# A Conformer kernel's opening: projection operands without the inverse root, root applied to the results, loads reordered, own taps in two banks

## Chip, cores, metric

The kernel runs on one core of one Trainium2 chip. Times are device microseconds (us) of one execution; the number that counts is the median of several runs. The profile is one further execution, recorded by the hardware profiler; its span goes from the first to the last instruction.

Engines: TensorE (PE, its weight loads PEld), VectorE (DVE), ScalarE (ACT), GpSimd (POOL) and SyncE (SP, which issues the transfers here).

## The reference, cut

Two blocks run one after the other on x of 512 tokens by 1024 features. All that the change touches is the first mixer of the first block, a Conformer convolution behind an RMS norm:

```python
u = rms_norm(h, conv_norm_g)                        # x * rsqrt(mean(x*x) + eps) * g
a = u @ w_pw1 + b_pw1                               # 1024 -> 2048
u = a[..., :D] * sigmoid(a[..., D:])                # gate
u = causal_depthwise_conv(u, dw_w, width 31) + dw_b
u = silu(layer_norm(u, ln_g, ln_b))
h = h + u @ w_pw2 + b_pw2
...                                                 # FFN, gate by projection, attention, second block
```

The root, rsqrt(mean(x*x) + eps), is one number for each token.

## The kernel before

Data lies transposed: features on the 128 partitions, tokens along the 512 columns, so x is 8 chunks of 128 x 512 (`h`). A float32 product is made of three matmuls in a faster format: each operand is cut into a rounded high part and the remainder as low part, and the product is high x high + low x high + high x low (lines 733, 734, 735). ACT rounds weights and operands, POOL subtracts for the low part of weights, DVE for the low part of operands.

Weights stream through a ring of four slots (`weight_raw`), 1 MB each. Slot j of `pw1` holds, for output chunk j, 128 columns for the value and 128 for the gate: two tiles of 8 x 3 matmuls each, in PSUM banks (`conv_tile`). Bank t is written again only when `tile_used` says so.

The opening, before: SP loads the 8 chunks of x, with the constants among them, then the params, then the first slots. ACT squares each chunk (line 3057), DVE adds the squares (2179), PE sums them over the partitions with a matmul against ones (904), ACT makes the inverse root with Ln and Exp (2709, 2712). Then `rms_apply`: for each chunk DVE multiplies h, gain and root into PSUM (1600), ACT rounds that to `u_hi` (2648), DVE subtracts for `u_lo` (1585, one operand in PSUM). PE starts on a chunk as its `u_lo` is there. While it waits, PE runs filler matmuls on constants (`keep_at_work`, line 1331) and small products for an attention bias table and a scalar lambda, whose results DVE copies out (2189 to 2195).

The convolution, 31 taps a channel, is split over engines for each chunk c: PE does 12 taps (16 in the last chunk) with diagonal weights (1352), on shifted copies that SP makes by DMA from the gated chunk (610); POOL builds the diagonals (2540). DVE does 12 own taps (10 in the last) in a chain in PSUM bank 6 (2236, 2238). ACT scales by a tap and POOL adds for the other 7 (5), the side taps (3105, 3110, 2536). For each chunk:

- ACT's sigmoid of the gate tile (2841), then DVE's gate (2222), which frees the two banks and lets SP, ACT and DVE start on the chunk;
- ACT's rounding of the slot after next (2640) and POOL's low half of it (2499);
- inside the next chunk's own taps, behind the fourth, DVE's sum of the three shares (`conv_finish`, 2247, 2249), which ACT squares for the layer norm (3090) and DVE adds up (2207, 2209).

Each engine works through its instructions in the order of the program; semaphores order them among each other. `link` makes DVE wait for the instruction just issued before it goes on; `link(..., 1)` lets one stay open.

Of the kernel before, what the change touches and what calls it, by code (L numbers as in the profile page):

```python
# [22 lines left out]
P = 128  # L23
# [27 lines left out]
BANKS = 4  # L51
HALF = P // 2
# [9 lines left out]
    ("conv_norm_g", 8), ("conv_b_pw1", 16), ("conv_dw_w", 8 * (CONV - OWN_FROM)), ("conv_tap_rows", SHIFTS * sum(TAP_GROUPS)), ("conv_dw_b", 8),  # L62
    ("conv_ln_g", 8), ("conv_ln_b", 8), ("conv_b_pw2", 8), ("attn_norm_g", 8),
    ("q_norm_g", 1), ("k_norm_g", 1), ("sub_norm_g", 1), ("lambda", 4),
# [5 lines left out]
for _name, _w in PARAM_WIDTHS:  # L70
    PARAM_AT[_name] = _n
    _n += _w
N_PARAMS = _n

CONST_WIDTHS = [("ident", P), ("flip", P), ("ones", P), ("ones64", P), ("key_fold", P), ("chunkmask", P),
                ("ahead", P), ("first_counts", 64), ("fold", 32), ("spread", QUARTER), ("eps", 2), ("zero", 1)]
# [4 lines left out]
N_CONSTS = _n  # L81
LATE_WIDTH = HEADS * P + 2 * S
# [151 lines left out]
def build(nc, a, out):  # L234
    stages, landed_due, tiles_after, split_no, slot_width, hi_free = plan_slots()
    n_slots = len(slot_width)
    with ExitStack() as ctx:
# [126 lines left out]
        diagonals = arena[:, DC * S:DC * S + group_base[DC] * P]  # L364
        side_base = [sum(SIDE_TAPS[:c]) for c in range(DC)]
# [5 lines left out]
        def conv_tile(t):  # L371

            return ps[:, t % BANKS]

# [47 lines left out]
        par_landed, con_landed = sem("par_landed"), sem("con_landed")  # L422
        p_landed = sem("p_landed")
# [114 lines left out]
        def _(sp):  # L538
            n = Tally()
            for c in range(DC):  # L540
                sp.dma_start(chunk(h, c), a["x_t"][c * P:(c + 1) * P]).then_inc(x_landed[c], 16)
                if c == 3:
                    sp.dma_start(con[:], a["consts"]).then_inc(con_landed, 16)
            sp.dma_start(par[:], a["params"]).then_inc(par_landed, 16)
# [47 lines left out]
            for j in range(RING):  # L592
                load("pw1", pair(a["conv_w_pw1"], a["conv_w_pw1"], 0, D), only=j)
                if j == 0:
                    sp.dma_start(v_sb[0:BUCKETS, 0:HEADS], a["rel_bias"]).then_inc(inputs_landed, 16)
                    sp.dma_start(v_sb[0:BUCKETS + 1, 8:648], a["bucket_of"]).then_inc(inputs_landed, 16)

            sp.wait_ge(bias_sb, 1)
            sp.dma_start(bias_rows, act[0:HEADS, 20 * S:20 * S + 640]).then_inc(bias_stored, 16)
# [12 lines left out]
            for c in range(DC):  # L612
                shift_copies(c)
                if c < DC - RING:
# [91 lines left out]
        def _(pe):  # L706
            n = Tally()
            pe.sem_inc(tile_used, BANKS)
            pe.wait_ge(con_landed, 16)
# [623 lines left out]
            keep_at_work(2, ps[:, 1])  # L1333
            rms_stat(adds=8)
            keep_at_work(3, ps[:, 1])
# [219 lines left out]
        def _(dve):  # L1555
# [671 lines left out]
            def conv_taps(c):  # L2227
# [13 lines left out]
                if c:  # L2241
                    square_sum(c - 1)
# [1166 lines left out]
```

## Time and profile before

| | |
|---|---|
| median of 3 runs | 2500.81 us (2500.45 to 2500.85) |
| the profiled execution's own time | 2501.13 us |
| its span | 2499.1 us |
| busy share PE / PEld | 98% / 79% |
| busy share DVE / ACT / POOL | 54% / 40% / 44% |
| HBM read | 269.72 MB, 109 GB/s over the span |

A row of the timeline gives the start, the time that it covers, engine, line, operation, tile written <- tiles read, how many instructions, and in brackets how long the engine sat idle before it and what released it. Busy times of PE overlap, since matmuls are pipelined.

### The profile page before, as it was taken

To read this page: it belongs to the slowest core of one execution; us is meant where nothing else is said; L and a number is where in the kernel's file an instruction comes from. 1 tells how busy PE (TensorE), PEld (TensorE's weight loads), DVE (VectorE), ACT (ScalarE), POOL (GpSimd) and SP (SyncE) were. 2 spreads that over 40 slices of the span, in tenths; PEclk is the share of its full clock that TensorE was granted. 3 is DMA by queue.
4 is the path that set the end of the run, shared out by engine and by line. 5 is a ranking of instruction groups with operands and counts; after the bars stand their busy time and mean duration, and the time that the engine had idled before them with its cause. 6 is when DMAs were issued, how large, how long until landed. Compare 5 with 4: busy or idle time off the path is not lost.

```text
span 2499.1 us, 31843 instructions
## 1 busy us (share of the span) xinstructions
PE 2457.9 (98%) x11794; PEld 1971.9 (79%) x11794; DVE 1355.7 (54%) x2128; ACT 987.5 (40%) x1386; POOL 1100.4 (44%) x555
## 2 busy tenths in 40 slices
PE   8999999999999999999999999999999999999998
PEld 5768888887777788888877878888888758888887
DVE  7856635635566465365338655551554465652553
ACT  5553222235565432223334254532344243532333
POOL 6944444444332344444443413544444313544443
PEclk9999999999999999999999999999999999999999
DMA  7635546533322364564352312324332222324322
GB/s 191 164 88 174 186 142 202 164 89 110 94 71 72 82 213 161 167 190 136 93 145 85 101 35 76 92 76 117 95 87 91 64 68 68 85 80 114 99 76 70
DMA packets 403321, 282.06 MB, mean 113 GB/s; under 512 B 10707, under 2 KB 382419, under 8 KB 403196
## 3 DMA queue, kind: packets, MB, share of 16 engines
q1 hardware_dynamic: 389372, 230.06, 32.7%
q10 hardware_dynamic: 13824, 50.34, 5.4%
q8 instruction: 77, 1.26, 0.2%
q14 instruction: 48, 0.39, 0.0%
HBM read 269.72 MB, written 2.12 MB: 109 GB/s over the span
## 4 chain that ended last, share of the span: by engine, by line
PE 91%; DVE 4%; ACT 3%; issue 1%; POOL 1%; DMA 1%; SPq 0%; DVEq 0%; ACTq 0%
PE ps L733 27%; PE ps L735 27%; PE ps L734 27%; PE ps L1511 1%; PE ps L1352 1%; PE ps L1120 1%; PE ps L1094 1%; PE ps L1233 1%; PE ps L1079 1%; PE ps L1082 1%; PE ps L1208 1%; DVE u_lo L1689 1%; PE ps L1453 0%; ACT weight_hi L2640 0%; PE ps L1222 0%
## 5 line engine op out<-in xcount | busy, mean ns | idle before, releaser
L2499 POOL TENSOR_TENSOR weight_lo<-weight_raw,weight_hi 128x1024 fp32r<-128x1024 f32 (+3 forms) x417 | 944.0, 2285 | 1315.3 <-ACT weight_hi L2640 1191.5
L735 PE MATMUL ps<-u_hi,weight_lo 128*128 128x512 f32 (+1 forms) x2456 | 929.7, 379 | 0.0
L733 PE MATMUL ps<-u_hi,weight_hi 128*128 128x512 f32 (+1 forms) x2248 | 879.6, 391 | 9.1 <-DVE u_lo L1585 2.2
L734 PE MATMUL ps<-u_lo,weight_hi 128*128 128x512 f32 (+1 forms) x2248 | 869.5, 387 | 0.0
L2640 ACT ACTIVATE weight_hi<-weight_raw 128x2048 fp32r<-128x2048 f32 (+2 forms) x213 | 363.1, 1705 | 571.4 <-PE ps L735 539.9
L735 PEld LDWEIGHTS ps<-u_hi,weight_lo 128*128 128x128 f32 x2456 | 462.1, 188 | 86.3
L733 PEld LDWEIGHTS ps<-u_hi,weight_hi 128*128 128x128 f32 x2248 | 422.4, 188 | 117.7 <-issue 15.8
L734 PEld LDWEIGHTS ps<-u_lo,weight_hi 128*128 128x128 f32 x2248 | 422.5, 188 | 86.2 <-issue 2.9
L735 PE MATMUL ps<-act_hi,weight_lo 128*128 128x512 f32 (+1 forms) x748 | 282.0, 377 | 0.0
L733 PE MATMUL ps<-act_hi,weight_hi 128*128 128x512 f32 (+1 forms) x704 | 269.8, 383 | 0.0
L734 PE MATMUL ps<-act_lo,weight_hi 128*128 128x512 f32 (+1 forms) x704 | 269.5, 383 | 0.0
L1585 DVE TENSOR_TENSOR act_lo<-tmp,act_hi 128x512 f32 (+1 forms) x88 | 160.4, 1823 | 98.4 <-ACT act_hi L2648 98.4
L1925 DVE SCALAR_TENSOR_TENSOR tmp<-ps,par,tmp 128x510 f32<-128x510 f32 (+1 forms) x176 | 119.7, 743 | 153.5 <-ACT tmp L2901 153.5
L735 PEld LDWEIGHTS ps<-act_hi,weight_lo 128*128 128x128 f32 x748 | 140.7, 188 | 25.6
L734 PEld LDWEIGHTS ps<-act_lo,weight_hi 128*128 128x128 f32 x704 | 132.4, 188 | 25.9
L733 PEld LDWEIGHTS ps<-act_hi,weight_hi 128*128 128x128 f32 x704 | 132.4, 188 | 25.8
L1854 DVE SCALAR_TENSOR_TENSOR ps<-arena,small,ps 128x512 f32<-128x512 f32 x168 | 118.7, 752 | 33.3 <-DMA arena<-in_ada_w 26.6
L2901 ACT ACTIVATE tmp<-ps,par 128x512 f32<-128x512 f32 x88 | 59.5, 681 | 166.3 <-PE ps L735 166.3
L2850 ACT ACTIVATE tmp<-tmp 128x512 f32<-128x512 f32 x60 | 37.9, 632 | 201.2 <-DVE tmp L1885 141.5
L1804 DVE TENSOR_TENSOR ps<-ps,tmp 128x512 f32<-128x512 f32 x32 | 22.4, 700 | 130.4 <-PE ps L735 130.4
L2648 ACT ACTIVATE act_hi<-tmp 128x512 f32 (+1 forms) x88 | 55.1, 626 | 82.8 <-DVE tmp L1932 62.1
L1932 DVE TENSOR_TENSOR tmp<-tmp 128x512 f32<-128x512 f32 x44 | 55.2, 1256 | 34.1 <-ACT tmp L2906 34.1
(335 smaller groups left out, 2683.7 us busy)
## 6 DMA issues: line engine op xcount, KB each, us to landing
weight_raw<-in_ffn_w_up SPq DMA_DIRECT2D x132, 512.0 KB, 5.2
arena<-in_ada_w ACTq DMA_DIRECT2D x96, 512.0 KB, 5.8
weight_raw<-in_ffn_w_down SPq DMA_DIRECT2D x64, 704.0 KB, 4.6
weight_raw<-in_ffn_w_gate SPq DMA_DIRECT2D x44, 512.0 KB, 4.0
weight_raw<-in_ev_w_in SPq DMA_DIRECT2D x10, 1024.0 KB, 5.6
weight_raw<-in_conv_w_pw SPq DMA_DIRECT2D x16, 512.0 KB, 6.6
weight_raw<-in_ple_w_gate SPq DMA_DIRECT2D x16, 512.0 KB, 3.8
weight_raw<-in_attn_w_qkv SPq DMA_DIRECT2D x16, 512.0 KB, 5.2
```

Of the source, the lines that this page charges most:

```text
L733: pe.matmul(bank, w[0], x[0], start=start, stop=False)
L734: pe.matmul(bank, w[0], x[1], start=False, stop=False)
L735: return pe.matmul(bank, w[1], x[0], start=False, stop=stop)
L1585: dve.tensor_tensor(lo, t, hi.bitcast(F32), ALU.subtract).then_inc(x_ready, 1)
L1854: ada_link(dve.scalar_tensor_tensor(acc, row, by, acc, ALU.mult, ALU.add), 1 - z)
L1925: link(dve.scalar_tensor_tensor(y[:, back:], bank[:, 0:S - back], tap, y[:, back:], ALU.mult, ALU.add), spare)
L1932: dve.tensor_tensor(sq[par_], act_tmp[par_], rinv[par_], ALU.mult).then_inc(t_ready, 1)
L2499: low_part = pool.tensor_tensor(w_lo[r][:, cols], raw[r][:, cols], w_hi(k0 + j)[:, cols].bitcast(F32), ALU.subtract)
L2640: sc.activation(w_hi(slot)[:, 0:width], raw[slot % RING][:, 0:width], ACT.Copy).then_inc(w_rounded, 1)
L2648: sc.activation(dst, src, ACT.Copy).then_inc(hi_done, 1)
L2850: sc.activation(t, t, func).then_inc(act_done, 1)
L2901: sc.activation(y, bank, ACT.Copy, scale=tap).then_inc(act_done, 1)
```

## The change

What it does:

- **Operands.** `u_hi` is h times gain, rounded by ACT straight from h; `u_lo` is h times gain less `u_hi`, by DVE. Neither needs the root. Squares and their sum go on beside them, the running sum in PSUM.
- **Root on results.** PE sums the squares after chunk 0's products; ACT makes the root into SBUF. DVE multiplies both tiles of each chunk by it (`conv_scale`): the gate tile goes to SBUF, where ACT takes the sigmoid, the value tile stays in its bank. The biases still come after that, in sigmoid and gate.
- **Weights and loads.** Halves of slot 0 and 1 land on semaphores of their own and are rounded and split as they come; chunk 0 and 1's first tiles run their matmuls with high weights before those with low weights. SP's order is: a first cut of the params, first half slot, two chunks of x, a first cut of the constants, chunk 2, second half slot, the other chunks, slot 1, then the rest of params and constants.
- **Own taps** alternate between PSUM banks 6 and 3, with one instruction left open, and are added at the end. So the projection's tiles use three banks instead of four.
- **Moved**: the bias products behind chunk 1's tiles on PE, their copies behind the own taps of chunk 0 on DVE; lambda's product first on PE; all filler matmuls ahead of the products go; POOL builds two tables of diagonals ahead of the loop instead of five, and one in each of six rounds instead of three.

The diff, cut to its core:

```diff
-            for c in range(DC):
+            def input_chunk(c):
                 sp.dma_start(chunk(h, c), a["x_t"][c * P:(c + 1) * P]).then_inc(x_landed[c], 16)
...
+            sp.dma_start(par[:, 0:PARAMS_FIRST], a["params"][:, 0:PARAMS_FIRST]).then_inc(par_first_landed, 16)
+            half_slot(0, 0)
+            input_chunk(0)
+            input_chunk(1)
+            sp.dma_start(con[:, 0:CONSTS_FIRST], a["consts"][:, 0:CONSTS_FIRST]).then_inc(ones_landed, 16)
+            input_chunk(2)
+            half_slot(0, 1)
+            for c in range(3, DC):
+                input_chunk(c)
+            half_slot(1, 0)
+            half_slot(1, 1)
+            sp.dma_start(par[:, PARAMS_FIRST:], a["params"][:, PARAMS_FIRST:]).then_inc(par_landed, 16)
+            sp.dma_start(con[:, CONSTS_FIRST:], a["consts"][:, CONSTS_FIRST:]).then_inc(con_landed, 16)
...
-            keep_at_work(2, ps[:, 1])
-            rms_stat(adds=8)
-            keep_at_work(3, ps[:, 1])
...
+                pe.wait_ge(first_rounded, 1)
                 for k in range(DC):
                     pe.wait_ge(x_ready, n.next(x_ready))
-                    if k == 0:
+                    high_passes(0, 0, k)
+                    if k == 3:
+                        pe.wait_ge(w_rounded, 1)
+                        for q in range(3):
+                            high_passes(0, 1, q)
                         pe.wait_ge(first_low, 1)
-                    first_product(0, k)
-                    if k == 3:
-                        slot_of("pw1", Step(0))
                         for q in range(3):
-                            first_product(1, q)
+                            low_pass(0, 0, q)
                     if k >= 3:
-                        first_product(1, k)
-                pe.wait_ge(lam_exp, 1)
-                pe.wait_ge(bias_sb, 1)
+                        high_passes(0, 1, k)
+                        low_pass(0, 0, k)
+                    if k == 6:
+                        pe.wait_ge(w_ready, 1)
+                        for q in range(6):
+                            low_pass(0, 1, q)
+                    if k >= 6:
+                        low_pass(0, 1, k)
+                rms_stat(adds=8)
...
+            for c in range(DC):
+                dve.wait_ge(hi_done, i0 + c + 1)
+                dve.scalar_tensor_tensor(chunk(u_lo, c), chunk(h, c), pcol("conv_norm_g", c), chunk(u_hi, c).bitcast(F32),
+                                         ALU.mult, ALU.subtract).then_inc(x_ready, 1)
+                dve.wait_ge(squared, q0 + c + 1)
+                if c == 0:
+                    dve.tensor_copy(square_sum_bank, sq[0]).then_inc(summed, 1)
+                else:
+                    dve.wait_ge(summed, c)
+                    dve.tensor_tensor(sum2 if c == DC - 1 else square_sum_bank, square_sum_bank, sq[c % 2], ALU.add).then_inc(summed, 1)
...
+            def conv_scale(c):
+
+                dve.wait_ge(tile_done, t0 + 2 * c + 2)
+                dve.tensor_tensor(act_tmp[c % 2], conv_tile(2 * c + 1), rinv[0], ALU.mult).then_inc(conv_scaled, 1)
+                link(dve.tensor_tensor(conv_tile(2 * c), conv_tile(2 * c), rinv[0], ALU.mult))
...
-                own, y = ps[:, 6], chunk(conv_out, c)
-                for t in taps:
-                    x = cin[:, t:t + S]
-                    if t == taps[0]:
-                        link(dve.tensor_scalar(own, x, tap(t), None, ALU.mult))
+                own, y = (ps[:, 6], ps[:, 3]), chunk(conv_out, c)
+                for k, t in enumerate(taps):
+                    x, acc = cin[:, t:t + S], own[k % 2]
+                    last = t == taps[-1]
+                    if k < 2:
+                        link(dve.tensor_scalar(acc, x, tap(t), None, ALU.mult), 1)
                     else:
-                        link(dve.scalar_tensor_tensor(y if t == taps[-1] else own, x, tap(t), own, ALU.mult, ALU.add))
-                    if t == taps[3] and c:
+                        link(dve.scalar_tensor_tensor(y if last else acc, x, tap(t), acc, ALU.mult, ALU.add), 0 if last else 1)
+                    if k == 3 and c:
                         conv_finish(c - 1)
                 if c:
                     square_sum(c - 1)
+                if c < DC - 1:
+                    conv_scale(c + 1)
+                link(dve.tensor_tensor(y, own[len(taps) % 2], y, ALU.add))
...
+            split_half(0, 0)
+            sc.wait_ge(par_first_landed, 16)
             for c in range(DC):
                 sc.wait_ge(x_landed[c], 16)
+                sc.activation(chunk(u_hi, c), chunk(h, c), ACT.Copy, scale=pcol("conv_norm_g", c)).then_inc(hi_done, 1)
                 if c >= 2:
                     sc.wait_ge(summed, c - 1)
                 sc.activation(sq[c % 2], chunk(h, c), ACT.Square).then_inc(squared, 1)
+                if c == 2:
+                    split_half(0, 1)
...
+            split_half(1, 0)
             link.begin(0)
             sc.wait_ge(stat_done, n.next(stat_done))
...
+            inverse_root(ps[:, 4], 1.0 / D, eps_rms, rinv[0])
+            split_half(1, 1)
```

Where the order of instructions changes, at three places. In the names, `weight_raw_49` and `_51` are slots 0 and 1, `weight_hi_57` and `_58` the two buffers of rounded weights, `weight_lo_50` and on the low parts; `tmp`, `act`, `arena` are working tiles, `small` and `par` columns of scalars.

ACT in the opening before, from the root to the first rounding of a whole slot:

```order
L2709 ACTIVATE tmp<-ps,con 128x512
L2712 ACTIVATE ps<-tmp 128x512
L3066 ACTIVATE weight_hi_57<-weight_raw_49 128x1024
L2648 ACTIVATE u_hi<-ps 128x512
L3066 ACTIVATE weight_hi_57<-weight_raw_49 128x1024
...
L2648 ACTIVATE u_hi<-ps 128x512 x3
L3082 ACTIVATE small<-ps 128x2
L2841 ACT_TABLE_LOAD
L2841 ACTIVATE tmp<-ps,par 128x512
L2640 ACTIVATE weight_hi_57<-weight_raw_53 128x2048
```

ACT there in the changed kernel, from the last chunk of x on (what it waits for in brackets):

```order
L3114 ACTIVATE u_hi<-h,par 128x512 [waits x_landed7]
L3117 ACTIVATE tmp<-h 128x512 [waits summed]
L3122 ACTIVATE small<-ps 128x2 [waits lam_mm]
L3108 ACTIVATE weight_hi_58<-weight_raw_51 128x1024 [waits half_landed1]
L2768 ACTIVATE tmp<-ps,con 128x512 [waits stat_done]
L2771 ACTIVATE tmp<-tmp 128x512 [waits a_chain]
L3108 ACTIVATE weight_hi_58<-weight_raw_51 128x1024 [waits weights_landed1]
L2889 ACT_TABLE_LOAD
L2889 ACTIVATE tmp<-tmp,par 128x512 [waits conv_scaled]
L2699 ACTIVATE weight_hi_57<-weight_raw_53 128x2048 [waits weights_landed2,tile_done,par_landed]
```

The root (2768, 2771) has moved behind the operands of all chunks; a half of slot 1 and the table load now stand between it and the first sigmoid.

DVE, in chunk 1's round before, from the sums of chunk 0 to the gate of chunk 2:

```order
L2247 TENSOR_TENSOR ps<-ps,arena 128x512 [waits pe_taps_done,d_chain]
L2249 TENSOR_TENSOR arena<-ps,act 128x512 [waits side_added,d_chain]
L2238 SCALAR_TENSOR_TENSOR ps<-act,par,ps 128x512 [waits d_chain] x7
L2238 SCALAR_TENSOR_TENSOR arena<-act,par,ps 128x512 [waits d_chain]
L2207 COPY ps<-tmp 128x512 [waits squared,d_chain]
L2222 SCALAR_TENSOR_TENSOR act<-ps,par,tmp 128x512 [waits d_chain,act_done,tile_done]
```

And in the changed kernel:

```order
L2301 TENSOR_TENSOR ps<-ps,arena 128x512 [waits pe_taps_done,d_chain]
L2303 TENSOR_TENSOR arena<-ps,act 128x512 [waits side_added,d_chain]
L2289 SCALAR_TENSOR_TENSOR ps<-act,par,ps 128x512 [waits d_chain] x7
L2289 SCALAR_TENSOR_TENSOR arena<-act,par,ps 128x512 [waits d_chain]
L2252 COPY ps<-tmp 128x512 [waits squared,d_chain]
L2262 TENSOR_TENSOR tmp<-ps,tmp 128x512 [waits d_chain,tile_done]
L2263 TENSOR_TENSOR ps<-ps,tmp 128x512
L2296 TENSOR_TENSOR arena<-ps,arena 128x512 [waits d_chain]
L2272 SCALAR_TENSOR_TENSOR act<-ps,par,tmp 128x512 [waits act_done,d_chain]
```

Two scalings (2262, 2263) and the sum of the two banks (2296) are new ahead of the gate; the wait for PE's tiles has moved from the gate to the first scaling.

POOL ahead of the rounds and in the first, before:

```order
L2547 TENSOR_TENSOR weight_lo_50<-weight_raw_49,weight_hi_57 128x1024 x2
L2540 TENSOR_TENSOR arena<-con,par 128x384 x2
L2499 TENSOR_TENSOR weight_lo_52<-weight_raw_51,weight_hi_58 128x2048
L2540 TENSOR_TENSOR arena<-con,par 128x384 x3
L2499 TENSOR_TENSOR weight_lo_54<-weight_raw_53,weight_hi_57 128x2048
L2536 TENSOR_TENSOR act<-act 128x512 x6
L2499 TENSOR_TENSOR weight_lo_56<-weight_raw_55,weight_hi_58 128x2048
```

And in the changed kernel:

```order
L2608 TENSOR_TENSOR weight_lo_50<-weight_raw_49,weight_hi_57 128x1024 x2
L2608 TENSOR_TENSOR weight_lo_52<-weight_raw_51,weight_hi_58 128x1024 x2
L2600 TENSOR_TENSOR arena<-con,par 128x384 x2
L2559 TENSOR_TENSOR weight_lo_54<-weight_raw_53,weight_hi_57 128x2048
L2596 TENSOR_TENSOR act<-act 128x512 x6
L2600 TENSOR_TENSOR arena<-con,par 128x384
L2559 TENSOR_TENSOR weight_lo_56<-weight_raw_55,weight_hi_58 128x2048
```

Three of the tables (2540, now 2600) have moved from ahead of the first round into rounds.

## Rows read from the trace of the kernel before

**Rows 1.** The page's head.

```profile
span 2499.1 us, 31843 instructions
```

**Rows 2.** Timeline of the opening: start, us covered, engine, line, operation.

```profile
0.75 1.28 ACT L2652 ACT_TABLE_LOAD   x1 [0.75 <-PEq L3400]
...
3.46 1.27 ACT L3057 ACTIVATE tmp<-h 128x512 f32<-128x512 f32 x2 [1.43 <-DMA h<-in_x_t]
...
13.71 0.69 ACT L2709 ACTIVATE tmp<-ps,con 128x512 f32<-128x512 f32 x1 [2.12 <-PE ps L904]
...
15.49 1.06 ACT L3066 ACTIVATE weight_hi<-weight_raw 128x1024 fp32r<-128x1024 f32 x1 [0.46 <-DMA weight_raw<-in_conv_w_pw]
...
16.62 4.71 POOL L2547 TENSOR_TENSOR weight_lo<-weight_raw,weight_hi 128x1024 fp32r<-128x1024 f32 x2 [16.17 <-ACT weight_hi L3066]
...
19.12 0.47 PE L733 MATMUL ps<-u_hi,weight_hi 128*128 128x512 f32 x1 [0.21 <-POOL weight_lo L2547]
...
27.23 0.67 DVE L2189 COPY act<-ps 8x512 f32<-8x512 f32 x1
...
29.13 0.15 DVE L2195 TENSOR_SCALAR small<-par 128x1 f32<-128x1 f32 x1
```

**Rows 3.** Timeline of DVE in the convolution's rounds.

```profile
32.49 0.75 DVE L2222 SCALAR_TENSOR_TENSOR act<-ps,par,tmp 128x512 f32<-128x512 f32 x1 [2.73 <-ACT tmp L2841]
...
44.89 0.75 DVE L2222 SCALAR_TENSOR_TENSOR act<-ps,par,tmp 128x512 f32<-128x512 f32 x1 [1.95 <-ACT tmp L2841]
45.90 0.76 DVE L2236 TENSOR_SCALAR ps<-act,par 128x512 f32<-128x512 f32 x1 [0.26 <-DVE act L2222]
...
50.83 5.50 DVE L2238 SCALAR_TENSOR_TENSOR ps<-act,par,ps 128x512 f32<-128x512 f32 x7 [0.34 <-DVE arena L2249]
...
59.06 0.75 DVE L2236 TENSOR_SCALAR ps<-act,par 128x512 f32<-128x512 f32 x1 [0.24 <-DVE act L2222]
...
126.33 0.75 DVE L2222 SCALAR_TENSOR_TENSOR act<-ps,par,tmp 128x512 f32<-128x512 f32 x1 [0.92 <-ACT tmp L2841]
```

**Rows 4.** Timeline of POOL in the same rounds.

```profile
34.23 4.62 POOL L2499 TENSOR_TENSOR weight_lo<-weight_raw,weight_hi 128x2048 fp32r<-128x2048 f32 x1 [3.76 <-ACT weight_hi L2640]
38.82 8.49 POOL L2536 TENSOR_TENSOR act<-act 128x512 f32<-128x512 f32 x6
...
60.31 0.84 POOL L2540 TENSOR_TENSOR arena<-con,par 128x384 f32<-128x384 f32 x1
```

**Rows 5.** Timelines of ACT, PE and DVE at the end of the convolution.

```profile
125.54 0.69 ACT L2841 ACTIVATE tmp<-ps,par 128x512 f32<-128x512 f32 x1 [1.00 <-PE ps L735]
...
135.50 3.64 PE L1352 MATMUL ps<-act,arena 128*32 128x512 f32 x32 [1.07 <-DMA act<-act]
...
139.21 0.70 DVE L2247 TENSOR_TENSOR ps<-ps,arena 128x512 f32<-128x512 f32 x1 [1.53 <-PE ps L1352]
```

**Rows 6.** Timeline of DVE elsewhere: neighbours that don't wait for each other.

```profile
195.60 0.70 DVE L1580 TENSOR_TENSOR ps<-ps,tmp 128x512 f32<-128x512 f32 x1
196.21 0.75 DVE L1816 SCALAR_TENSOR_TENSOR u_lo<-h,par,u_hi 128x512 fp32r<-128x512 f32 x1
...
247.88 1.41 DVE L1854 SCALAR_TENSOR_TENSOR ps<-arena,small,ps 128x512 f32<-128x512 f32 x2 [0.15 <-DVE ps L1852]
```

**Rows 7.** Timelines of POOL and DVE where line 1816 meets a split.

```profile
185.80 5.23 POOL L2499 TENSOR_TENSOR weight_lo<-weight_raw,weight_hi 128x1024 fp32r<-128x1024 f32 x2 [6.26 <-ACT weight_hi L2640]
...
186.89 1.88 DVE L1816 SCALAR_TENSOR_TENSOR u_lo<-h,par,u_hi 128x512 fp32r<-128x512 f32 x1
...
188.70 2.89 DVE L1816 SCALAR_TENSOR_TENSOR u_lo<-h,par,u_hi 128x512 fp32r<-128x512 f32 x1
```

**Rows 8.** Fillers on PE, ns min/median/max; one product in the chain that ended last.

```profile
L1331 PE MATMUL ps<-con x12: 592/593/1219, 8.1 to 18.3; 128*128 128x512 f32 x12
...
30.95 0.23 PE ps L733
```

**Rows 9.** Stretches: busy us of the engines, clock, DMA share, GB/s.

```profile
16.00:22.00 6.00, 5.41 (x18) 2.41 (x17) 5.77 (x10) 4.80 (x8) 5.38 (x3) 1.00 1.19 290
```

More of the change, by code:

```diff
@@ new lines, in conv_slots @@
+                        low_pass(0, 0, k)
[6 more added lines that the diff above has]
+                rms_stat(adds=8)
+                pe.wait_ge(first_rounded, 2)
+                for k in range(DC):
+                    high_passes(1, 0, k)
+                pe.wait_ge(first_low, 2)
+                for k in range(DC):
+                    low_pass(1, 0, k)
@@ L2712, in inverse_root @@
                 sc.activation(to if root is None else root, to, ACT.Exp, scale=-0.5).then_inc(done, 1)
-            def rms():
-                link.begin(0)
-                sc.wait_ge(stat_done, n.next(stat_done))
-                inverse_root(ps[:, 4], 1.0 / D, eps_rms, rinv[0])
-                n.take(x_ready, DC)
-                for c in range(DC):
-                    sc.wait_ge(t_ready, n.next(t_ready))
-                    high(chunk(u_hi, c), sq[c % 2])
             def ln(eps, src, func, gain, shift):
@@ L3057, in _ @@
                 sc.activation(sq[c % 2], chunk(h, c), ACT.Square).then_inc(squared, 1)
+                if c == 2:
+                    split_half(0, 1)
+            n.take(x_ready, DC)
+            sc.wait_ge(lam_mm, 1)
+            sc.activation(lam[:, 2:4], ps[:, 3, 0:2], ACT.Exp).then_inc(lam_exp, 1)
+            split_half(1, 0)
             link.begin(0)
             sc.wait_ge(stat_done, n.next(stat_done))
-            sc.wait_ge(con_landed, 16)
-            inverse_root(ps[:, 4], 1.0 / D, eps_rms, sum1, root=ps[:, 5])
-            def split_half(slot, z, done=None):
-                cols = slice(z * SLOT // 2, (z + 1) * SLOT // 2)
-                sc.wait_ge(landed[slot], landed_due[slot])
-                half = sc.activation(w_hi(slot)[:, cols], raw[slot][:, cols], ACT.Copy)
-                if done is not None:
-                    half.then_inc(done, 1)
-            split_half(0, 0, first_rounded)
-            n.take(x_ready, DC)
-            for c in range(DC):
-                sc.wait_ge(t_ready, n.next(t_ready))
-                high(chunk(u_hi, c), ps[:, 6 + c % 2])
-                if c == 0:
-                    split_half(0, 1, w_rounded)
-                if c == 2:
-                    split_half(1, 0)
-                if c == 4:
-                    split_half(1, 1, w_rounded)
-            sc.wait_ge(bias_mm, 1)
-            sc.activation(lam[:, 2:4], ps[:, 3, 0:2], ACT.Exp).then_inc(lam_exp, 1)
+            inverse_root(ps[:, 4], 1.0 / D, eps_rms, rinv[0])
+            split_half(1, 1)
             s0 = n.take(summed, DC - 1)
```

171 lines of the change are left out of this document (94 added, 77 removed).

## The prediction, on record before the result

> **What bounds the kernel now.** I read the page first: one core, a span of 2499.1 us [rows 1], TensorE (PE) busy for 98% of it. The diff ends with the Conformer convolution, about the first 140 us; nothing behind it changes but its place in time. So I read that stretch engine by engine, and the reader should see two things.
>
> First, the opening. The first product starts at 19.12 us [rows 2], behind squares, the inverse root on ScalarE (ACT) and a scaled copy per chunk. That is the idle time the change goes for.
>
> Second, what follows. From the gate of chunk 0 at 32.49 to that of chunk 7 at 126.33 [rows 3] the stage is a relay over four engines, each nearly full. PE needs 48 products of 0.23 us [rows 8] and 24 taps a chunk (32 of them took 3.64 [rows 5], so 2.7), 13.8. POOL needs a split (4.6), six side sums (8.45) and in some chunks a table of diagonals (0.8): 13.05 to 13.85 [rows 4]. VectorE (DVE) needs 13.16 where it waited for nothing (45.90 to 59.06) [rows 3]. The mean round was (126.33 - 44.89)/6 = 13.57. An opening that is 10 us shorter is therefore worth 10 us only if DVE and POOL start 10 us earlier too and need no more per chunk.
>
> After the gate of chunk 7 come the shifted copies, PE's last taps at 135.50 (1.07 us of waiting for DMA) and the last sum at 139.21 [rows 5]: 12.9 us behind the gate. The change leaves that tail alone, so **I forecast the gate of chunk 7** and carry its shift to the end. Its sigmoid waited 1.00 us for PE [rows 5]: PE is the bound there today.
>
> **The opening, step by step.** The first half slot of weights now goes ahead of x. Chunk 0 of x, first in the queue today, was being read at 3.46 [rows 2]. The half slot is 512 KB where that chunk is 256, and weights moved at 290 GB/s [rows 9]: 0.9 us more, and some 0.7 for the small transfer ahead of it and its shorter rows. That makes 5.1 us, an estimate; the bounds are 4.1 (no transfer in the way) and 8 (it lands no sooner than a later transfer does under load). ACT rounds it in 1.06 [rows 2]: 6.2. POOL then takes 2.36 for the low half (4.71 for two) [rows 2]: until 8.55.
>
> Here is the first catch. Before, DVE's low part of the operand read PSUM and one SBUF tile. Now it reads h and u_hi, both in SBUF, in the form of line 1816. Where that form met POOL's split (POOL from 185.80), it took 1.88 and 2.89 us and ended after each POOL instruction [rows 7]; alone it takes 0.75 [rows 6]. I take it as blocked: u_lo(0) ends at 9.3, and the first product starts there, 9.8 us earlier than today. (Bounds: never blocked, start 8.0.) DVE then spends 0.67 + 0.61 a chunk [rows 6]: u_lo(2) ends at 11.7. POOL's second half runs 11.7 to 14.05, and u_lo(3) is blocked again, to 14.85. u_lo(7) ends near 20.
>
> The second catch: until u_lo(3), PE has only 6 of chunk 0's 48 products to do; 42 remain, 42 x 0.23 = 9.7 us, to 24.5. The filler matmuls that ran ahead of the products are gone. Today the first of those lasted 1219 ns and the rest 592 [rows 8]: PE's first work after idling ran at half rate, 1.2 instead of 2.4 GHz, though the clock column does not show it. I charge 8 of the 42 at twice 0.23 (nearest row: about four such fillers), +1.6, hence 26.1; bounds 0 and 20 of them (+4).
>
> Only then comes the sum over partitions, since PE does chunk 0's products first: two matmuls of the fillers' kind (592 ns each, overlapping [rows 8]), 1.0 to 27.1; Ln and Exp at 0.69 [rows 2], 28.5. ACT then has the second half of slot 1 to round (1.0, to 29.5) and the table load of the sigmoid, 1.28 [rows 2], which today falls into an idle stretch: 30.7. DVE's scaling of both tiles (1.3) hides under those. Sigmoid 0.69, gate of chunk 0 at **31.4, against 32.49**. Of 9.8 us, 1.1 are left.
>
> **The rounds.** DVE's own taps alternate between two banks. In one bank each waits for the one before: 5.50 us for seven, 0.79 apart [rows 3]. Two of the same form on two banks took 1.41 together [rows 6], so 0.67 apart; that pair is the nearest row and I take it (bounds 0.61 and 0.79). Eleven gaps a chunk shrink by 0.12: -1.3. Added a chunk: two scalings, 0.61 + 0.73 (the second is waited for), and the sum of the two banks, 0.73: +2.07. DVE's round becomes 13.16 - 1.3 + 2.07 = 13.9.
>
> Chunk 0: gate 31.4, taps begin 1.0 later as today, 11 x 0.67 + 0.79 = 8.2 to 40.6, scalings 1.3, sum 0.73, and the bias copies, which ran 27.23 to 29.28 in idle time [rows 2] and now stand ahead of the gate, 2.05: gate of chunk 1 at 44.75, against 44.89 [rows 3]. Six rounds of 13.9: gate of chunk 7 at 128.15, against 126.33. **The sum is +1.8 us**, or +0.2 with the clock up at once.
>
> Cover for the rest: PE is no longer in the way. Chunk 1's tiles end near 38, its taps of chunk 0 at 42.6 once the copies land, and with 13.8 a chunk it has chunk 7's tiles at about 123, three before DVE asks. The move to three banks costs nothing while PE leads thus. POOL begins slot 2 at 33.6 (ACT's split behind the sigmoid), 34.23 today after 3.76 of waiting [rows 4]; but three diagonal tables that were built in that gap now stand inside the loop, +2.4. Its rounds are 13.85: chunk 6's sums start at 33.6 + 4.6 + 6 x 13.85 = 121.3 and end at 129.8. ACT's last product for them is released three adds of 1.42 earlier, 125.6, with sigmoid 7 behind it to 126.9: 1.2 us of slack before the gate. So POOL is a second bound, nearly as late as DVE: a faster DVE alone gains at most those 1.2 us. Reordered params and constants land by 20 (5.2 MB ahead at 290 GB/s from about 2 us on [rows 9]) and are needed at 30; moved bias products cost PE 1 us under its lead.
>
> The profiled execution took 2501.13 with 2.0 us outside its span; the runs' median is 2500.81. 2501.13 + 1.8 gives 2502.9, less 0.3 for the median, **2502.6 us**.
>
> **A rule against the change.** The two banks rest on 1.41 for a pair [rows 6]. The Trainium skill, page VectorE: DVE Perf Modes, section The DRAIN you can't avoid, says that the next op starts only when the pipe is empty, and that leaving out semaphores doesn't shorten that. By it the second bank would gain nothing. The pair here speaks against it; if it held, the time would be that of the third rival.
>
> **The rivals.**
> - *The forecast*: DVE's round and the late root eat the gain; 2502.6, its own range 2500 to 2506. Chance 0.63.
> - *Faster opening*: u_lo isn't held by POOL, PE is at full clock, the half slot lands 1 us sooner. u_lo(3) ends at 11.3, PE's products near 21, gate of chunk 0 at 26.3. POOL's chain, from about 28.4, then binds: gate of chunk 7 at 28.4 + 4.6 + 83.1 + 4.3 + 1.3 = 121.7 at best, -4.6. For it: POOL's own 185.80 row is only one meeting. Against it: both instructions there were late. 2496 to 2500; chance 0.15. Beyond -5 it would need POOL's rounds shorter as well, by moving 2.4 us of tables into slack that isn't there.
> - *Two banks don't overlap*: the taps stay 0.79 apart, DVE's round is 15.2, and 1.3 us more in chunk 0: 44.75 + 1.3 + 6 x 15.2 = 137.3, +11, so 2512. Slower is decided from a gap of about 0.72 on (5 us = 0.05 x 11 x 7 plus the 1.8). Against it: the pair; for it: an additional tile to finish, and the waits between. Chance 0.12.
> - *Late first weights*: the half slot shares its engines with x and lands 2 to 3 us later, and PE stays at half rate through most of chunk 0. All behind shifts: 2505 to 2508. Chance 0.10.
>
> **Numbers.** From no change a measurement of this kernel can tell about 0.2%, 5 us: below 2495.8 or above 2505.8. Faster 0.07 (the end of the second case and what I don't see), same 0.78, slower 0.15 (the third case and part of the last). The range of eight in ten leaves out the third rival and the far end of the second: 2498 to 2508.
>
> **What would show it.** In the profile after: first product near 9 us, u_lo of 2 us or more beside POOL's halves, the statistic near 26, gate of chunk 0 near 31, chunk 1's near 45, rounds of 13.9 on DVE with hardly a wait for PE, PE with some idle before the shifted copies, POOL full. The forecast is wrong if DVE's low parts run through POOL's splits, if own taps stand 0.6 or 0.79 apart, or if the first half slot lands far from 5 us.

## The result, and the profile after

The changed kernel takes 2504.51 us (median of 20 runs, 2502.60 to 2506.65), the kernel before 2500.65 (20 runs, 2500.17 to 2502.21): a ratio of 1.0015, 95% interval 1.0008 to 1.0022. It is 3.9 us slower and inside the range. The profiled run is the fastest of the 20: 2502.60, with a span of 2500.6 [rows 1]. A profile shows one run, so where the other 2 us of the median went can't be read from it.

The opening of the changed kernel, engine by engine (start, us covered, engine, line, operation, and in brackets the idle time before it and what ended it):

```profile
5.25 1.06 ACT L3108 ACTIVATE weight_hi<-weight_raw 128x1024 fp32r<-128x1024 f32 x1 [3.22 <-DMA weight_raw<-in_conv_w_pw]
...
6.38 2.36 POOL L2608 TENSOR_TENSOR weight_lo<-weight_raw,weight_hi 128x1024 fp32r<-128x1024 f32 x1 [5.94 <-ACT weight_hi L3108]
11.59 2.45 POOL L2608 TENSOR_TENSOR weight_lo<-weight_raw,weight_hi 128x1024 fp32r<-128x1024 f32 x1 [2.85 <-ACT weight_hi L3108]
...
7.04 2.25 DVE L2221 SCALAR_TENSOR_TENSOR u_lo<-h,par,u_hi 128x512 fp32r<-128x512 f32 x1 [3.54 <-ACT u_hi L3114]
12.33 2.25 DVE L2221 SCALAR_TENSOR_TENSOR u_lo<-h,par,u_hi 128x512 fp32r<-128x512 f32 x1
...
9.44 0.76 PE L1394 MATMUL ps<-u_hi,weight_hi 128*128 128x512 f32 x1 [1.87 <-DVE u_lo L2221]
14.64 0.79 PE L1394 MATMUL ps<-u_hi,weight_hi 128*128 128x512 f32 x1 [1.55 <-DVE u_lo L2221]
16.51 0.63 PE L1394 MATMUL ps<-u_hi,weight_hi 128*128 128x512 f32 x1
16.93 0.63 PE L1395 MATMUL ps<-u_lo,weight_hi 128*128 128x512 f32 x1
19.75 0.39 PE L1395 MATMUL ps<-u_lo,weight_hi 128*128 128x512 f32 x1
19.98 0.40 PE L1399 MATMUL ps<-u_hi,weight_lo 128*128 128x512 f32 x1
26.60 1.02 PE L930 MATMUL ps<-tmp,con 128*128 128x512 f32 x2
```

The first product starts at 9.44 instead of 19.12 [rows 2]. Both long u_lo end 0.55 us after the GpSimd split that runs beside them; the other six take 0.73 or 0.74. From 14.64 to 19.5 the products stand 0.43 apart, then 0.23. So the sum over partitions is taken at 26.60, and gate 0 comes only 0.4 us sooner than before [rows 3], as the timeline of VectorE shows:

```profile
32.09 0.75 DVE L2272 SCALAR_TENSOR_TENSOR act<-ps,par,tmp 128x512 f32<-128x512 f32 x1 [1.76 <-ACT tmp L2889]
...
43.32 0.68 DVE L2236 COPY act<-ps 8x512 f32<-8x512 f32 x1
44.03 0.28 DVE L2237 COPY act<-ps 8x128 f32<-8x128 f32 x1
44.35 1.25 DVE L2239 TENSOR_TENSOR small<-small 128x1 f32<-128x1 f32 x1
...
46.32 0.75 DVE L2272 SCALAR_TENSOR_TENSOR act<-ps,par,tmp 128x512 f32<-128x512 f32 x1 [0.35 <-DVE small L2241]
...
51.70 4.71 DVE L2289 SCALAR_TENSOR_TENSOR ps<-act,par,ps 128x512 f32<-128x512 f32 x7 [0.34 <-DVE arena L2303]
...
59.99 0.75 DVE L2272 SCALAR_TENSOR_TENSOR act<-ps,par,tmp 128x512 f32<-128x512 f32 x1
...
128.38 0.75 DVE L2272 SCALAR_TENSOR_TENSOR act<-ps,par,tmp 128x512 f32<-128x512 f32 x1
...
141.17 0.70 DVE L2301 TENSOR_TENSOR ps<-ps,arena 128x512 f32<-128x512 f32 x1 [1.70 <-PE ps L1378]
```

Seven own taps take 4.71 instead of 5.50 [rows 3]. Each round, gate to gate, is 13.68, six times. The last sum is 1.96 us later than in [rows 5]. In the table of waits over 44 to 127 us, VectorE waits for nobody but itself, and ScalarE's sigmoid waits for VectorE's scaling (us in total, times, longest):

```profile
DVE act L2272 <- DVE small L2241: 0.3, 1, 0.3
...
ACT tmp L2889 <- DVE tmp L2262: 4.5, 5, 1.4
```

### The profile page after: what moved, and what is told of

Same layout as the page of the kernel before. It is cut to its first block, busy times and chain, and to the rows that moved or that the text cites. A ratio compares the mean times of both kernels' runs of the same rounds, so it can differ in the third digit from the quotient of the medians.

```text
span 2500.6 us, 31829 instructions
## 1 busy us (share of the span) xinstructions
PE 2454.9 (98%) x11782; PEld 1971.0 (79%) x11782; DVE 1358.3 (54%) x2144; ACT 988.4 (40%) x1386; POOL 1101.2 (44%) x556
## 4 chain that ended last, share of the span: by engine, by line
PE 87%; DVE 7%; ACT 3%; issue 2%; POOL 1%; DMA 0%; SPq 0%; DVEq 0%; ACTq 0%
PE ps L759 26%; PE ps L760 26%; PE ps L761 26%; DVE ps L2289 1%; PE ps L1563 1%; PE ps L1146 1%; PE ps L1120 1%; PE ps L1259 1%; PE ps L1105 1%; PE ps L1108 1%; PE ps L1234 1%; DVE u_lo L1726 1%; PE ps L1505 0%; ACT weight_hi L2699 0%; DVE ps L2287 0%
## 5 line engine op out<-in xcount | busy, mean ns | idle before, releaser
L761 PE MATMUL ps<-u_hi,weight_lo 128*128 128x512 f32 (+1 forms) x2432 | 919.3, 378 | 0.0
L759 PE MATMUL ps<-u_hi,weight_hi 128*128 128x512 f32 (+1 forms) x2224 | 869.2, 391 | 8.5 <-POOL weight_lo L2559 2.0
L760 PE MATMUL ps<-u_lo,weight_hi 128*128 128x512 f32 (+1 forms) x2224 | 859.0, 386 | 0.0
L760 PEld LDWEIGHTS ps<-u_lo,weight_hi 128*128 128x128 f32 x2224 | 417.9, 188 | 85.2 <-issue 2.9
```

Source lines behind the costliest of these rows:

```text
L759: pe.matmul(bank, w[0], x[0], start=start, stop=False)
L760: pe.matmul(bank, w[0], x[1], start=False, stop=False)
L761: return pe.matmul(bank, w[1], x[0], start=False, stop=stop)
```

## The experiments

All but one are edits of the changed kernel, and all compute the reference in full; a filler is a matrix product whose result nobody reads. Medians are of 11 runs each (6 for the single bank). "Gate 7" and "last sum" are those of the profiled run, 128.38 and 141.17 in the changed kernel. The kernel before was run again beside each group of these runs and took 2500.64 to 2501.17, so a difference of half a microsecond between medians of different groups says nothing.

**The sum of squares ahead of the second tile's low products.**

```diff
+                    if k == DC - 1:
+                        rms_stat(adds=8)
+                        pe.wait_ge(w_ready, 1)
+                        for q in range(DC):
+                            low_pass(0, 1, q)
-                    if k == 6: ...
-                    if k >= 6: ...
-                rms_stat(adds=8)
```

> The sum of squares goes to TensorE as soon as it is made (20.2 us in the changed kernel's trace), ahead of the sixteen products that complete the second tile, instead of behind all of chunk 0's products (26.6 us). My theory (the convolution ends where VectorE's unbroken rounds of 13.68 us end, and these start at gate 0, which waits for the late root): root about 23, table load about 24 to 25, gate 0 at about 28.5 (was 32.09); gate 1 only 2 to 2.5 us earlier (it was 46.32), since TensorE's fourth tile, at 38.6, then holds the scaling; gate 7 at about 126 (was 128.38), median 2.0 to 2.5 us below the changed kernel's. Rival, TensorE's rounds (13.81 us) bind: gate 7 gains no more than 1 us. Rival, GpSimd's rounds (13.8 us) bind: its second-slot split moves forward with the root, so about 2 us too, but VectorE would then wait at its gates.

2502.91 (2501.88 to 2504.34), 1.6 below the changed kernel. The sum was taken at 24.73, not soon after 20.2, when its operand is made: TensorE, still behind its operands after the slow products, comes to it no sooner. Gate 0 stood at 30.23 (expected 28.5), gate 7 at 126.58, 1.8 sooner. The last sum stood at 140.85, only 0.3 sooner: something behind gate 7 took the rest.

**Bias copies on ScalarE, lambda operations in VectorE's last wait.**

```diff
-                if c == 0:
-                    bias_copies()
...
+            lambda_values()
             conv_finish(DC - 1)
...
+                    if i == 3 and c == 1:
+                        sc.wait_ge(bias_mm, 1)
+                        link(sc.activation(act[0:HEADS, 20 * S:21 * S], ps[0:HEADS, 7], ACT.Copy))
+                        sc.activation(act[0:HEADS, 21 * S:21 * S + P], ps[0:HEADS, 4, 0:P], ACT.Copy).then_inc(bias_sb, 1)
```

> The two copies of the bias products go from VectorE's path ahead of gate 1 to ScalarE, inside its side taps of chunk 1, and the three small operations on lambda to VectorE's wait for the last taps. My theory (VectorE's rounds bind from gate 0 on): gate 1 at 43.3 to 43.6 (was 46.32), gate 7 at 125.5 to 126.5 (was 128.38), median 2 to 3 us below the changed kernel's, or as much of that as TensorE's slack (about 1.7 us at the tiles of chunk 2) leaves. Rival, GpSimd binds: gate 1 earlier, but a wait of that size appears at gates 2 to 4, and gate 7 and the end stay within 0.5 us.

2504.02 (2503.34 to 2505.11). Gate 1 came at 44.55, yet gate 7 at 128.16: my theory missed, the rival holds (counted from gate 0, which was 0.36 later in this run, gate 7 gained 0.58). In the table of waits (44 to 127 us) ScalarE's wait for VectorE's scaling is gone: VectorE now waits for ScalarE, and ScalarE for nobody but GpSimd:

```profile
DVE ps L2252 <- ACT tmp L3132: 1.2, 4, 0.5
...
ACT act L3154 <- POOL act L2593: 36.9, 18, 5.6
```

**Fillers ahead of the first product.** Three of ones by ones, five on the half slot.

> TensorE is given matrix products without use from about 1.5 us on (three of ones by ones, then five on the first rounded half slot), up to the first product of the projection at 9.44 us; nothing else is changed. If the half rate of its first products (0.43 us apart until 19.3, 0.23 after) is what stands behind the late root: the products are 0.23 apart from the first on, the sum of squares is taken at 23 to 24 (was 26.6), gate 0 is at 29 to 30 (was 32.09), and the median is 1.5 to 2.5 us below, with a narrower spread of runs (the changed kernel's 20 runs lie 4 us apart, those before 2 us) if the spread comes from the moment at which the rate rises. Rival, the rate isn't set by what the engine did before, or the operands' arrival holds it: gate 0 within 0.5 us of 32.09 and the spread unchanged.

2502.58 (2500.95 to 2503.93), 1.9 below. No product stood 0.43 apart any more, but the fillers waited for the ones to land (7.39) and held the first product until 13.21, so the sum was taken at 24.97, gate 0 at 30.48 and gate 7 at 126.84. The runs still lay 3 us apart (4 in the changed kernel): the spread isn't made in the opening alone.

**One bank.** The own taps as in the kernel before, without the sum of two banks.

> VectorE's own taps go back into one bank, each waiting for the one before, without the sum of two banks at the end; the rest of the change stays. My theory (independent operations stand 0.66 apart, dependent ones 0.79, and VectorE's rounds bind): a round is 9 to 10 steps of 0.12 to 0.13 longer and one sum of 0.7 shorter, so 14.1 to 14.4 instead of 13.68, and gate 7 is 3 to 5 us later: median 3 to 5 us above the changed kernel's. Rival, two banks don't overlap: rounds 0.7 shorter, median up to 5 us lower. Rival, another engine binds: under 1 us of difference, with waits at the gates in the place of the difference.

2510.25 (2508.56 to 2510.87), 5.7 above. Seven taps took 5.50 again, and the round was 14.64: 0.96 longer, not the 0.4 to 0.7 that I expected: the taps cost 1.47 a round, and dropping the sum of the banks saved only 0.49 of its 0.73, since the gate then waits 0.25 for the scaling ahead of it. Two banks do overlap. The 5.7 us are not the rounds alone: this run's taps of chunk 7 took 6.50 us, for a reason that the next run shows.

**Two fillers ahead of the taps of chunk 7.** The run with the sum moved had shown where its gain went. TensorE's rows at the end of the convolution, first of the changed kernel, then of the one with the bias copies moved:

```profile
133.73 1.13 PE L936 MATMUL ps<-arena,con 128*128 128x512 f32 x2 [0.85 <-DVEq L2306]
137.38 3.64 PE L1378 MATMUL ps<-act,arena 128*32 128x512 f32 x32 [2.52 <-DMA act<-act]
```

```profile
133.49 1.13 PE L936 MATMUL ps<-arena,con 128*128 128x512 f32 x2 [0.35 <-DVEq L2304]
137.27 6.48 PE L1378 MATMUL ps<-act,arena 128*32 128x512 f32 x32 [2.65 <-DMA act<-act]
```

The same 32 taps took 3.64 and 6.48. The stretches of the second one give the reason (us, PE busy with its count, granted clock, DMA share, GB/s):

```profile
128.00:135.00 7.00, 6.27 (x14) 1.00 0.58 120
135.00:139.00 4.00, 1.73 (x11) 0.65 0.92 275
139.00:143.00 4.00, 4.00 (x24) 0.50 0.49 181
```

The clock fell to its lower level, 1.2 of 2.4 GHz, in TensorE's wait for the shifted copies, and the taps ran at it.

```diff
                 chunk_sums(0, DC - 1)
+                keep_at_work(2, ps[:, 1])
                 pe_taps(DC - 1)
```

> The changed kernel with two matrix products without use between TensorE's last chunk sum and its taps of chunk 7 (where it waited 2.52 us for the shifted copies, after 0.85 us ahead of that sum); nothing else is changed. Theory A: in most runs, though not in the changed kernel's profiled one (the fastest of its 20), TensorE's granted clock falls during this wait, as it shows in the profiles of four experiments (0.50 to 0.71 there, and the 32 taps take 5.2 to 6.5 us instead of 3.64). Then the clock stays at 1.00, the taps take 3.6 to 3.7 us, the last sum follows gate 7 by 12.8 us, and the median falls to 2502.3 to 2503.2 (from 2504.5), with the runs within about 2 us of each other. Theory B: the spread comes from elsewhere (the opening's clock, the landing of transfers): median within 0.5 us of 2504.5, runs 4 us apart.

2503.15 (2502.18 to 2504.74), 1.4 below the changed kernel, runs 2.6 us apart. The clock stayed at 1.00, the taps took 3.64, the last sum came 12.74 behind gate 7. Theory A.

**The same two fillers in the kernel before.**

> The kernel before with the same two products without use ahead of the taps of chunk 7. There TensorE waited 1.07 us in that place, and its taps ran at the full clock. Theory A: little or nothing to gain, 0 to 0.7 us, so the difference between this one and the changed kernel with the same products is that of VectorE's rounds alone, about 2 us. Theory B: no difference for either.

2501.59 (2500.98 to 2503.12) against 2500.82 (2499.61 to 2502.68): nothing to gain there; the 0.8 more lies inside the interval of the ratio (0.9994 to 1.0012). Its TensorE waits 1.07 us in that place [rows 5].

**Tables ahead.** GpSimd builds five ahead of the loop again.

> GpSimd builds five of the tap tables ahead of the loop, as the kernel before did, and the last three behind the sums of chunks 1 to 3; nothing else is changed. Theory (GpSimd's rounds of 13.8 us don't hold the end; VectorE's of 13.68 do, and TensorE's of 13.81 are next): its split of the second slot begins some 2.5 us later (was 34.00) and TensorE's tiles of chunk 2 or 3 may wait for it by up to 1 us, which VectorE's slack at the tiles covers; gate 7 within 0.3 us of 128.38, and the median within 0.7 us of 2504.5. Rival (GpSimd binds): the two tables moved out of the later rounds bring chunk 6's sums forward by 1 to 2 us and the end with them, or its later start sets the tiles back and the end by 1 to 2.5 us.

2505.03 (2503.34 to 2505.52), gate 7 at 128.61, both as my theory had it. The split of slot 2 began at 36.01, gate 1 waited 1.51 for its sigmoid, and VectorE's rounds went on from there.

**All of these together,** with fillers from 1.5 us on and the last half slot's rounding ahead of the root.

> The changed kernel with all that the runs so far favour: products without use on TensorE from 1.5 us to the first product, without the wait for the ones ahead of them (four of ones by ones, three on the first rounded half slot), the sum of squares behind the last chunk's first five products, the last half slot's rounding ahead of the root, the bias copies on ScalarE with the three small lambda operations in VectorE's last wait, and two products without use ahead of the taps of chunk 7. Theory (three engines have almost the same round: VectorE 13.68, GpSimd 13.8, TensorE 13.81; each of these edits alone meets the next engine, together they move all three): first products 0.23 apart from 9.5 on, sum of squares at about 21, gate 0 at 25.5 to 27, gate 1 at 38.5 to 40.5, gate 7 at 121 to 123.5 with TensorE's rounds as the bound, last sum 12.8 us behind it, at 134 to 136 (before 139.21, changed 141.17); median 2496 to 2498.5, below both kernels. Rival (the arrival of the weights holds the tiles of chunks 1 to 3 once the engines are earlier): gate 7 not before 125, median 2499.5 to 2501.

2504.27 (2501.41 to 2504.82): a miss, gate 0 at 31.96. Three of the 11 runs took 2501.4 to 2501.6, the others 2504.0 to 2504.8. The stretches of the opening of one of the latter (columns as above):

```profile
8.00:12.00 4.00, 2.77 (x10) 1.00 1.08 372
12.00:14.00 2.00, 0.73 (x2) 1.00 1.16 316
14.00:16.00 2.00, 0.82 (x2) 0.58 1.18 302
16.00:20.00 4.00, 4.00 (x10) 0.50 1.10 332
...
22.00:24.00 2.00, 2.00 (x10) 1.00 1.20 290
```

The fillers had brought the clock up, and it fell again while operands came one by one, the last wait 2.05 us for u_lo of chunk 3. At the other end the subtraction for lambda took 2.72 us in VectorE's last wait, and the last sum came 14.24 behind gate 7. What ran beside it was a GpSimd split, not a sum as a later expectation says; the two end within 0.02 us of each other:

```profile
138.64 2.72 DVE L2246 TENSOR_TENSOR small<-small 128x1 f32<-128x1 f32 x1
...
136.78 4.56 POOL L2566 TENSOR_TENSOR weight_lo<-weight_raw,weight_hi 128x2048 fp32r<-128x2048 f32 x1 [0.77 <-ACT weight_hi L2706]
```

**Fillers ahead of the taps of chunk 0 as well** (six of 0.23 us, and the two ahead of chunk 7's).

> The changed kernel with the two products without use ahead of the taps of chunk 7, as in the run with these alone (median 2503.15), and six of 0.23 us ahead of the taps of chunk 0, where TensorE waits 1.8 us and where the granted clock fell in three of the profiles (0.88 to 0.91 over 42 to 56 us). Theory: both places of the lost clock are covered; the 24 taps of chunk 0 take 2.78 us, gate 7 follows gate 0 by 96.3 us, and the median is 2502.3 to 2503.0. Rival: what is lost at the taps of chunk 0 is covered by TensorE's slack later: median as in the run with the last fillers alone, 2503.15 within 0.3.

2502.68 (2500.36 to 2503.86). The taps took 2.78 and 3.64, gate 7 came 96.34 behind gate 0. Against 2503.15 that is 0.5, which two medians with this spread don't settle.

**The filled opening alone,** with 3, 3 and 8 fillers behind the products of chunks 0 to 2.

> Only the opening is filled: products without use on TensorE from 1.5 us to the first product (without the wait for the ones), and 3, 3 and 8 of them behind the products of chunks 0, 1 and 2, where TensorE otherwise waits for the next operands (in the run with all edits the granted clock rose, fell to 0.50 at 14 us behind a wait of 2.05 us, and came back at 21). Theory: clock 1.00 from 9 us on, no product 0.43 apart, sum of squares at 21.5 to 23 (was 26.60), gate 0 at 27 to 28.5 (was 32.09); gate 1 at 41 to 43, gate 7 at 123.5 to 126, as TensorE's rounds (13.81) let it; median 2500 to 2502. Rival: the clock falls all the same, gate 0 within 1 us of 32.

2502.30 (2501.54 to 2504.15), 2.2 below. The clock held (1.00 in every stretch to 26 us) and no product was 0.43 apart, but gate 0 stood at 30.34 (expected 27 to 28.5), since the sum came at 24.83, not 21.5 to 23: u_lo of chunk 3 still ended at 15, and TensorE had 42 products to do from there. Gate 7 was at 126.29. The taps of chunk 7 took 5.91 at a clock of 0.50, behind 3.33 us of waiting: an earlier convolution loses more there.

**All, mended.** The edits of the run with all together, the filled opening just shown, and four fillers ahead of the taps of chunk 0. The subtraction is written as an operation on one tensor and stands in VectorE's wait for the root:

```diff
-                link(dve.tensor_tensor(lam[:, 4:5], lam[:, 3:4], lam[:, 2:3], ALU.subtract))
+                link(dve.tensor_scalar(lam[:, 4:5], lam[:, 3:4], lam[:, 2:3], None, ALU.subtract))
```

> The filled opening (with the fillers between the first chunks' products), the sum of squares behind the last chunk's first five products, the last half slot's rounding ahead of the root, the bias copies on ScalarE, the lambda operations in VectorE's wait for the root with the subtraction as an operation on one tensor (as one on two tensors it took 2.72 us in VectorE's last wait, next to a running GpSimd sum), four fillers ahead of the taps of chunk 0 and two ahead of those of chunk 7. Theory: sum of squares at 20.5 to 21.5, gate 0 at 25.5 to 27, gate 1 at 38 to 40, then TensorE's rounds of 13.81: gate 7 at 120.5 to 123, last sum at 133 to 136 (before 139.21), median 2495.5 to 2498.5, 2 to 5 us below the kernel before. Rival: the weights of the later slots or GpSimd hold the tiles, gate 7 not before 124.5, median 2499 to 2501.

2498.51 (2497.93 to 2500.05) against 2500.64: ratio 0.9990, 0.9981 to 0.9999. Gate 0 at 28.82, gate 7 at 124.38, last sum at 137.18: less than expected, with gate 7 close to the rival's 124.5 (GpSimd holds it, as the table below shows), but below both kernels. The subtraction took 0.21, beside a running split.

**And the second half's low part behind the last u_lo.**

```diff
                     pool.wait_ge(rounded, j + 1)
+                    if z and not j:
+                        pool.wait_ge(x_ready, DC)
```

> The version with all edits (median 2498.51) with one more: GpSimd takes the low part of the second half slot only once VectorE has written the last of u_lo, so that u_lo of chunk 3 runs beside no GpSimd operation; TensorE takes the eight low products of the second tile last, behind the sum of squares, and has 3 instead of 8 products without use behind chunk 2. Theory (the 2.25 to 2.31 us of u_lo of chunk 0 and of chunk 3, against 0.73 of the others, are a wait for the GpSimd operation that runs beside them): u_lo of chunk 3 takes 0.73 and ends at 13.2 (was 14.78), u_lo of chunk 7 at 18.3 (was 19.8), u_lo of chunk 0 stays at 2.25; the sum of squares is taken at 21 to 22 (was 24.27), gate 0 is at 25.5 to 27 (was 28.82), and TensorE ends chunk 0's products at about 24 (was 25.2), which carries 1 us to the end: median 2497 to 2498. Rival (a wait of its own, such as the landing of chunk 3, sets those 2.25 us): u_lo of chunk 3 stays at 2.2 us and the median goes up by the second half's delay, to 2499 or more.

**2496.50** (2496.29 to 2497.48) against 2500.79 (2500.39 to 2502.83): ratio 0.9982, 0.9973 to 0.9991. It is 8 us below the changed kernel and 4.3 below the one before, with the narrowest spread of all. VectorE's u_lo of chunks 0 and 3, and its waits over 44 to 127 us:

```profile
7.47 2.27 DVE L2232 SCALAR_TENSOR_TENSOR u_lo<-h,par,u_hi 128x512 fp32r<-128x512 f32 x1 [4.00 <-ACT u_hi L3124]
...
12.78 0.73 DVE L2232 SCALAR_TENSOR_TENSOR u_lo<-h,par,u_hi 128x512 fp32r<-128x512 f32 x1
```

```profile
DVE tmp L2270 <- PE ps L761: 2.3, 4, 1.4
```

With no split beside it, u_lo of chunk 3 takes 0.73; chunk 0's, which still has one, 2.27. The run also moves the second tile's eight low products behind the sum of squares, so the 2.0 us against the run before it belong to both. The sum was taken at 21.41, gate 0 was at 25.96, gate 7 at 122.58. VectorE now waits for TensorE's tiles.

## Why the prediction came out as it did

**Three chains set gate 7.** In every version that keeps the changed kernel's work in its rounds, gate 7 is the latest of three sums: VectorE's, gate 1 and six rounds of 13.68 (82.1); GpSimd's, its split of slot 2 and 93.8; TensorE's, its taps of chunk 0 (plus what the clock cost them beyond 2.78) and 85.2. The first constant is from the changed kernel, the second from the run with the bias copies moved, the third from the last run; the other rows test them. The starts for the changed kernel:

```profile
34.00 4.63 POOL L2559 TENSOR_TENSOR weight_lo<-weight_raw,weight_hi 128x2048 fp32r<-128x2048 f32 x1
...
41.77 2.78 PE L1378 MATMUL ps<-act,arena 128*32 128x512 f32 x24 [1.83 <-DMA act<-act]
```

| version | VectorE | GpSimd | TensorE | gate 7 seen |
|---|---|---|---|---|
| changed kernel | **128.4** | 127.8 | 127.0 | 128.38 |
| sum of squares early | **126.6** | 125.9 | 124.8 | 126.58 |
| bias copies moved | 126.6 | **128.2** | 127.2 | 128.16 |
| fillers ahead of first product | 126.5 | 126.2 | **126.8** | 126.84 |
| two fillers ahead of chunk 7 | 127.9 | 127.4 | **128.2** | 128.16 |
| both places filled | **127.8** | 127.2 | 126.2 | 127.83 |
| all together | 126.0 | **127.5** | 126.3 | 127.53 |
| filled opening alone | **126.3** | 126.0 | 124.6 | 126.29 |
| all, mended | 122.9 | **124.4** | 123.8 | 124.38 |
| and the late half | 120.1 | 121.5 | **122.6** | 122.58 |

The runs with one bank and with five tables ahead have other rounds and aren't in it. The first product came 9.7 us sooner, but the three sums start hardly sooner than in the kernel before, or later: the split at 34.00 for 34.23, the taps at 41.77 for 42.44, gate 1 at 46.32 for 44.89. That is why the earlier start was worth nothing by itself, and why edits of one engine met the next.

**Step by step.** The half slot's landing (5.1, of which 0.7 rested on no row; ACT began at 5.25), u_lo(0) held to 9.3 (9.29), u_lo(3) to 14.85 (14.58), products to 26.1 (26.60, about 11 of them at half rate instead of 8), own taps 0.67 apart (0.66) and the round of 13.9 (13.68) came as worked out. Gate 0 was 0.7 late (32.09 for 31.4). The bias copies were mis-sized: 3.0 us with their gaps for 2.05, with 1.25 for the subtraction on two tensors beside GpSimd's sums, where it had taken 0.66 in the kernel before. Together gate 1 was 1.6 late (46.32 for 44.75), and six rounds 0.2 shorter each gave 1.3 back: gate 7 at 128.38 for 128.15. That the two misses nearly cancel is luck. (Two small sums of the prediction are off without changing it: its terms give 44.68 for gate 1, and 0.05 x 11 x 7 plus 1.8 is 5.65, not 5.) GpSimd, "a second bound" with 1.2 us of slack, had 0.6 by the table, and moving the bias copies gained just that between gate 0 and gate 7, though gate 7 itself came only 0.22 sooner.

**The step that failed** is "The change leaves that tail alone". TensorE "is no longer in the way" and so waits longer for the copies: 0.85 and 2.52 us, against 1.07. In that wait its clock can fall. Of the seven profiled versions without fillers there (the changed kernel among them), six lost the clock: their taps took 5.2 to 6.5 us, and the last sum came 14.3 to 15.9 us behind gate 7; only the changed kernel's own profile kept 12.8. With fillers there it was 12.7 to 12.8 in four of five profiles, the fifth having the slow subtraction. The medians agree: 2504.51, then 2503.15 with the last fillers and 2502.68 with both, which is near the 2502.6 of the forecast, and 2.0 us above its own runs of before, where +1.8 was forecast and the changed kernel measured +3.9. So the sum held up to gate 7, and the clock at the end adds most of what is missing. Shown is that filling the waits takes off 1.4 to 1.8 us of the median; that each single slow run of the changed kernel lost the clock there is argued, since only one of its runs has a trace. The mean granted clock of every run speaks for it: 0.999 in 4 of the changed kernel's 20 runs (2502.60 to 2503.80) and 0.997 or 0.998 in the others, but 0.999 in 9 of 11 with the last fillers and in all 11 with both. It doesn't say where the clock was lost, and the eight slowest runs (2505.71 and above, all at 0.998) aren't those with the lowest mean.

**The rivals.** The faster opening didn't come: POOL held u_lo and TensorE was at half rate. The last run, without the second hold and with the clock up, reached gate 0 at 25.96 and 2496.5, close to the 26.3 and 2496 to 2500 that this rival gave, but with the sum of squares and the bias copies moved as well. Two banks without overlap fell: one bank cost 5.7 us. The Trainium skill (VectorE: DVE Perf Modes, The DRAIN you can't avoid) also says that an operation that isn't held starts earlier, which the prediction left out; these runs agree with that: operations of 0.75 start 0.66 apart where the next need not wait, and 0.79 where it must. Late weights fell: they were 0.15 us late.

## What to carry to other kernels

Where several engines have almost the same round, write down each one's sum (its first start and its rounds) before pricing an edit: what an edit of one gains ends at the next sum, here after 0.6 us, and all had to move together for 8. Look for what a lead costs: an engine that comes early to its last piece of work waits there, and if that wait lowers its clock, the piece takes longer just where nothing hides it. And keep operations with two tensors in SBUF away from a GpSimd that works, on the path above all.

## What the chip showed unexpectedly

- TensorE's clock fell around waits of 2.1 to 3.7 us with little work beside them (0.50 to 0.81 in the stretches that hold the taps of chunk 7; with one bank the wait of 3.68 stood ahead of the last chunk sum, and the taps waited only 0.97), and once it had risen in the opening it fell again between sparse operands. In some profiles the taps of chunk 0, behind a wait of only 1.4 to 1.8 us, took 4.35 to 4.48 us instead of 2.78. Nearly the same wait kept the clock in one run (2.52 us) and lost it in another (2.49), so it adds to the spread; how much of the spread it makes is not shown.
- The clock's column is no proof of the full rate: in the changed kernel it shows 1.00 over 14.00 to 19.50, where the products stand 0.43 apart; in the run of all edits it shows 0.50 for that spacing.
- An operation on one column of two SBUF tensors took 1.25 us beside GpSimd's sums and 2.72 beside a split, and 0.21 beside a split with the second tensor given as a scalar operand. The Trainium skill (SBUF — State Buffer, Who interferes with whom) states that two SBUF inputs on VectorE contend with a GpSimd instruction that reads SBUF; u_lo of chunk 3, 2.25 beside a split and 0.73 without, agrees.
